# Attention written for both heads of a pair, with fixed PSUM banks and one maximum and exponential over all keys

## The reference

```python
sc = jnp.einsum('bqhd,bkhd->bhqk', qblk, k, preferred_element_type=jnp.float32) * scale
p = jax.nn.softmax(sc, axis=-1).astype(v.dtype)
return jnp.einsum('bhqk,bkhd->bqhd', p, v)
```

## The kernel before, in words

| Stage | Heads, in pairs | Keys | Rows of a score matmul | Units |
|---|---|---|---|---|
| 1, `attn` | 8 as (0,4), (1,5), (2,6), (3,7) | 512 | 64, in the lower or upper half of the partitions | 32 |
| 2, `ca` | 4, alone | 256 | 128 | 16 |
| 3, `mla` | 8 in pairs | 512 + 256 | 96 | 32 |
| 4, `na` | 8 in pairs | 512 + 256 | 64, lower or upper half | 32 |

## Time and profile before

### The profile page before, as it was taken

One profiled execution on the slowest core, in us unless ns is written; L12 is line 12 of the kernel. 1 busy time (PEld: TensorE's weight loads), 2 busy tenths in 40 slices (PEclk: granted clock), 3 DMA queues, 4 the chain that ended last, 5 costly groups with the idle time before them and its releaser, 6 DMA issues.

```text
span 2101.5 us, 21475 instructions
## 1 busy us (share of the span) xinstructions
PE 1892.6 (90%) x8510; PEld 1051.3 (50%) x8510; DVE 676.8 (32%) x1363; ACT 515.6 (25%) x1113; POOL 293.6 (14%) x132
## 2 busy tenths in 40 slices
PE   7999989986989798898979798886999999999988
PEld 5886334464343242434333242423955489546876
DVE  2594765354020100202020110205357500760054
ACT  4242341242010000100010000004346522654231
POOL 2322640300000000000000000002200042004460
PEclk9997799998999999999999999998699999999998
DMA  6230204524999999999999999994210072102131
GB/s 229 65 118 36 80 30 170 167 76 201 424 422 421 421 421 421 421 424 423 424 421 421 421 422 420 424 423 184 81 40 1 5 106 81 41 1 91 41 120 40
DMA packets 97119, 482.15 MB, mean 229 GB/s; under 512 B 21572, under 2 KB 26020, under 8 KB 79648
## 3 DMA queue, kind: packets, MB, share of 16 engines
q1 hardware_dynamic: 96016, 478.84, 57.5%
q0 software_dynamic: 1040, 2.46, 0.6%
HBM read 477.22 MB, written 4.55 MB: 229 GB/s over the span
## 4 chain that ended last, share of the span: by engine, by line
PE 67%; DVE 12%; DMA 11%; SPq 5%; issue 2%; ACT 2%; DVEq 0%; ACTq 0%
PE psum L492 33%; PE psum L1558 14%; DMA ring<-in_expert_w_down 10%; PE psum L1578 7%; SPq L1497 5%; PE psum L1541 3%; PE psum L573 3%; PE psum L1587 3%; PE psum L2123 2%; DVE ring L633 1%; DVE work_area L884 1%; DVE work_area L989 1%; DMA ring<-in_w_mod 1%; DVE work_area L1630 1%; DMA ring<-in_ca_wo 0%
## 5 line engine op out<-in xcount | busy, mean ns | idle before, releaser
L1558 PE MATMUL psum<-ring,work_area 128*64 128x512 f32 x2048 | 448.1, 594 | 35.9 <-DMA ring<-in_expert_w_gu 28.1
L1558 PEld LDWEIGHTS psum<-ring,work_area 128*64 128x64 f32 x2048 | 148.0, 137 | 329.5 <-issue 277.1
L1578 PE MATMUL psum<-ring,work_area 128*64 128x512 f32 x1024 | 233.4, 607 | 26.2 <-DMA ring<-in_expert_w_down 24.2
L1647 DVE TENSOR_TENSOR work_area<-psum,work_area 128x512 f32<-128x512 f32 x32 | 20.6, 686 | 595.0 <-ACT work_area L1610 595.0
L492 PE MATMUL psum<-ring 128*64 128x512 f32 (+3 forms) x384 | 173.3, 597 | 5.3 <-DVE small L1031 2.7
L1578 PEld LDWEIGHTS psum<-ring,work_area 128*64 128x64 f32 x1024 | 74.1, 139 | 175.2 <-issue 147.0
L492 PE MATMUL psum<-ring,hn 128*128 128x512 f32 (+4 forms) x384 | 151.7, 532 | 3.5 <-ACT work_area L604 1.1
L1744 POOL TENSOR_TENSOR hn<-x_res,ring 128x1024 f32<-128x1024 f32 x3 | 7.0, 2362 | 1046.2 <-DVE x_res L1654 1046.2
L1698 POOL TENSOR_TENSOR block_lo<-ring,part_hi 128x1024 fp32r<-128x1024 f32 x36 | 85.9, 2394 | 407.4 <-ACT part_hi L1691 407.4
L1610 ACT ACTIVATE work_area<-psum 128x512 f32<-128x512 f32 x32 | 17.4, 595 | 485.6 <-PE psum L1558 485.6
L492 PEld LDWEIGHTS psum<-ring,hn 128*128 128x128 f32 (+2 forms) x384 | 67.7, 188 | 80.3 <-issue 72.5
(11 more groups left out here) (408 smaller groups left out, 2833.4 us busy)
## 6 DMA issues: line engine op xcount, KB each, us to landing
ring<-in_expert_w_gu SPq DMA_DIRECT2D x128, 2048.0 KB, 26.1
ring<-in_expert_w_down SPq DMA_DIRECT2D x64, 2048.0 KB, 22.7
ring<-in_w_in SPq DMA_DIRECT2D x12, 2048.0 KB, 7.9
ring<-in_w_mod SPq DMA_DIRECT2D x8, 1536.0 KB, 6.5
ring<-in_w_out SPq DMA_DIRECT2D x3, 2048.0 KB, 13.1
ring<-in_ca_wkv SPq DMA_DIRECT2D x1, 4096.0 KB, 16.5
work_area<-na_scratch SPq DMA_DIRECT2D x16, 224.0 KB, 6.7
ring<-in_w_in SPq DMA_DIRECT2D x3, 1024.0 KB, 18.1
```

The lines of the kernel that those rows point to most:

```text
L1558: ins = pe.matmul(psum[h * 64:(h + 1) * 64, c, :], xsT[:, k, e * CAP:(e + 1) * CAP], w[:, (2 * c + h) * BANK:(2 * c + h + 1) * BANK], star ...
L1578: ins = pe.matmul(psum[n * 64:(n + 1) * 64, 6, :], hidT[b][:, j, h, :], w[:, j, n * BANK:(n + 1) * BANK], start=(q == 0 and j == 0), stop= ...
```

## The change

The helper plans by pairs. Units alternate between the two heads of a pair, and a step O covers two blocks of queries of both heads (256 columns each) where it covered four blocks of one. PE writes the scores of both units of a pair segment by segment in turn (`scores_pe`), and the value products of both heads in turn, into the lower and the upper 64 partitions (`out_pe`). PSUM is no longer a circle: banks 0 to 3 hold scores, 4 to 6 turned weights, 7 the outputs. A unit with 768 keys takes two score banks, so two units fit, and two turning banks with three blocks each. The maximum and the exponential run once over the unit's whole width, across banks; in stage 4 the maximum and exponential keep their two parts, because of the bias. Semaphores for scores, exponentials, turns and copies take the place of the bank semaphores, and at its start each stage waits until banks 0 to 6 are drained. Stage 2 has single heads and so the same units as before.

```diff
@@ -49,7 +49,8 @@
 NSLOT = 8
 NEG = -1e30
 SMALL = 672
-O_LATER = 3
+O_LATER, LAG = 3, 3
+SCORE_BANKS, TURN_BANKS, OUT_BANK = 4, (4, 5, 6), 7
...
-        def plan_attention(heads, segs, nkt, lag):
-            units = [(c, j, qt) for c in range(len(heads)) for j in range(len(heads[c])) for qt in range(T)]
-            order, n_out = [], 0
...
+        def plan_attention(heads, width):
+            nj = len(heads[0])
+            quarter = T // nj
+            units = [(c, part * quarter + q, j) for c in range(len(heads)) for part in range(nj)
+                     for q in range(quarter) for j in range(nj)]
+            n, order, turned, n_out = len(units), [], 0, 0
+            for i in range(0, n + nj * LAG, nj):
+                order += [("S", u) for u in range(i, min(i + nj, n))]
+                while turned < min(i + nj - LAG, n) or (i + nj >= n + nj * LAG and turned < n):
+                    order.append(("T", turned))
+                    turned += 1
+                while (n_out + 1) * T + O_LATER <= turned or (turned == n and n_out < n // T):
                     order.append(("O", n_out))
                     n_out += 1
-            size = {"S": len(segs), "T": -(-nkt // 4), "O": 1}
-            return units, order, {(kind, i): list(B.take(size[kind])) for kind, i in order}
...
+            banks_each = -(-width // BANK)
+            n_scores, per_turn = SCORE_BANKS // banks_each, nkt // banks_each
+            starts = [sum(segs[:i]) for i in range(nseg)]
+            def score_at(u):
+                o = (u % n_scores) * banks_each * BANK
+                return flat[:, o:o + width]
+            def turn_at(m):
+                return psum[:, TURN_BANKS[m % len(TURN_BANKS)], 0:per_turn * P]
...
+            entry = [B.last(b) for b in range(OUT_BANK)]
+            g_out = [B.take_at(OUT_BANK) for n in range(len(units) // T)]
...
+            B.next = 0
+            def scores_pe(first):
+                for s in range(nseg):
+                    for u in range(first, first + nj):
+                        c, qt, j = units[u]
+                        if s == 0 and u >= n_scores:
+                            pe.wait_ge(exped, before + u - n_scores + 1)
+                        ins = pe.matmul(score_at(u)[:, starts[s]:starts[s] + segs[s]], q_at(heads[c][j], qt), k_at(heads[c][j], s),
+                                        start=True, stop=True)
+                        if s == nseg - 1:
+                            ins.then_inc(scored, 1)
+            def turn_pe(u):
+                pe.wait_ge(normed, before + u + 1)
+                for m in range(u * banks_each, (u + 1) * banks_each):
+                    if m >= len(TURN_BANKS):
+                        pe.wait_ge(taken, turns_before + m - len(TURN_BANKS) + 1)
+                    for k in range(per_turn):
+                        o = (m % banks_each * per_turn + k) * P
+                        ins = pe.transpose(turn_at(m)[:, k * P:(k + 1) * P], pbuf[u % np_][:, o:o + P], ident)
+                    ins.then_inc(turned, 1)
+            def out_pe(n):
+                g = g_out[n]
+                B.acquire(pe, g)
+                pe.wait_ge(taken, turns_before + (n + 1) * T * banks_each)
+                for k in range(nkt):
+                    for j in range(nj):
+                        c = units[n * T][0]
+                        ins = pe.matmul(B.at(g)[j * dv:(j + 1) * dv, 0:cols], v_at(heads[c][j], k),
+                                        turns_at(n)[:, j, k, :], start=(k == 0), stop=(k == nkt - 1), skip_group_check=True)
+                B.filled(ins, g)
...
+                        act.wait_ge(maxed, before + i + 1)
+                        p = pbuf[i % np_]
+                        if bias is None:
+                            if i >= np_:
+                                act.wait_ge(turned, turns_before + (i - np_ + 1) * banks_each)
+                            act.activation(p, score_at(i), ACT.Exp, bias=neg_max(i),
+                                           accum_out=sums(i)[:, 0:1]).then_inc(exped, 1)
...
+                        n, q, j = i // T, i % T // nj, i % nj
+                        if i % T == 0 and n >= len(ptbuf):
+                            B.full(act, g_out[n - len(ptbuf)])
+                        for m in range(banks_each):
+                            act.wait_ge(turned, turns_before + i * banks_each + m + 1)
+                            act.activation(turns_at(n)[:, j, m * per_turn:(m + 1) * per_turn, q * P:(q + 1) * P],
+                                           turn_at(i * banks_each + m).rearrange("p (k q) -> p k q", k=per_turn),
+                                           ACT.Identity).then_inc(taken, 1)
...
+                        c, qt, j = units[i]
+                        dve.wait_ge(scored, before + i + 1)
+                        if bias is None:
+                            dve.tensor_reduce(neg_max(i), score_at(i), AX, ALU.max, negate=True).then_inc(maxed, 1)
```

More of the change, by code:

```diff
@@ L97, in __init__, with take_at, last @@
         self.free_sem = [ctx.enter_context(nc.semaphore(f"bank_free{b}")) for b in range(NBANK)]
+        self.used = [0] * NBANK
         self.next = 0
     def take(self, n):
-        g = self.next
-        self.next += n
-        return range(g, g + n)
+        return [self.take_at(None) for _ in range(n)]
+    def take_at(self, bank):
+        if bank is None:
+            bank = self.next
+            self.next = (bank + 1) % NBANK
+        g = self.used[bank] * NBANK + bank
+        self.used[bank] += 1
+        return g
+    def last(self, bank):
+        return (self.used[bank] - 1) * NBANK + bank
     def at(self, g):
@@ new lines, in build, with attention @@
+        units_before, turn_count = [0], [0]
+        def attention(heads, segs, q_at, k_at, v_at, dv, pbuf, ptbuf, o_out, bias=None, besides={}):
+            width, nseg = sum(segs), len(segs)
+            nkt, np_ = width // P, len(pbuf)
+            nj, units, order = plan_attention(heads, width)
+            cols = S // nj
+            flat = psum[:].rearrange("p b c -> p (b c)")
+            banks_each = -(-width // BANK)
[6 more added lines that the diff above has]
+                return psum[:, TURN_BANKS[m % len(TURN_BANKS)], 0:per_turn * P]
+            scored, exped, maxed, normed = sem("at_scores"), sem("at_exp"), sem("at_max"), sem("at_weights")
+            turned, taken, exp_biased = sem("at_turned"), sem("at_taken"), sem("at_exp_biased")
+            before = units_before[0]
+            units_before[0] += len(units)
@@ L557, in on_pe @@
             def on_pe():
-                for s, n in ready:
-                    pe.wait_ge(s, n)
+                for g in entry:
+                    B.drained(pe, g)
                 for kind, i in order:
-                    gs = gid[kind, i]
                     if kind == "S":
-                        c, j, qt = units[i]
-                        for si, g in enumerate(gs):
-                            B.acquire(pe, g)
-                            B.filled(product(g, B.at(g)[:, 0:segs[si]], [(q_at(heads[c][j], qt), k_at(heads[c][j], si))]), g)
+                        if i % nj == 0:
+                            scores_pe(i)
@@ L608, in on_act @@
                     elif kind == "T":
[L609 to L619 removed]
+                        n, q, j = i // T, i % T // nj, i % nj
[6 more added lines that the diff above has]
+                                           ACT.Identity).then_inc(taken, 1)
             def on_dve():
                 def divide(i):
+                    dve.wait_ge(exped, before + i + 1)
+                    s = sums(i)[:, 0:1]
                     if bias is not None:
                         dve.wait_ge(exp_biased, i + 1)
[L626 to L629 removed]
                         link(dve.tensor_tensor(recip(i)[:, 0:1], sums(i)[:, 0:1], sums(i)[:, 1:2], ALU.add))
@@ L1526, in piece @@
             return slot(s)
-        before_experts = range(B.next - NBANK, B.next)
+        before_experts = [B.last(b) for b in range(NBANK)]
         def experts_pe():
```

121 lines of the change are left out of this document (34 added, 87 removed).

## The result

| | before | after |
|---|---|---|
| Median of 4 runs each | 2102.14 us (2100.62 to 2106.4) | 2176.23 us (2169.52 to 2182.35) |
| Span of the profiled execution | 2101.5 | 2176.4 |
| PE, DVE, ACT busy | 1892.6, 676.8, 515.6 | 1851.0, 655.0, 511.3 |
| Mean granted clock | 0.955 | 0.928 |

The account below looks back on a forecast made before the run. PE's own work was taken to bound stage 3, DVE's pace between O's stage 4, POOL parts of stage 1. Span 2101.5 + 30 (stages) + 38 (clock) = 2169.5, plus 0.65 to the median: 2170 us, range 2150 to 2195.

Parts of the forecast that it names:

- The closed loop: Stages 3 and 4: a pair's fourth turning group waits for ACT's copy of the first; 6.76 and 7.35 us a pair.
- Stage 3 +22: Stage 3 at unchanged clock: a period of 16.7 us against 13.28, so 22 us more in all.
- stage 4 +23: Stage 4 at unchanged clock: a period of 17.85 us against 14.45, so 23 us more in all.
- Stage 2's +0.5: Stage 2 keeps its units and pace; waiting for drained banks at the stages' starts adds 0.5 us.
- Clock +38: Stages 3 and 4: pauses in every pair lower PE's clock, costing 38 us, with ends 0 and 120.
- a third of the 120: Stages 3 and 4: share taken of the 120 us that running fully at 1.2 GHz would cost.
- The rival that the clock holds (2132): Stages 3 and 4: the pauses don't lower the clock, so only the +30 remains, 2132 us; chance 0.17.
- Stage 1 -15: Stage 1: no such loop, shorter periods in its free part and a shorter end; 15 us less.
- O and the scores: Column halves overlap in O (3.15 us, stages 3 and 4); row halves in scores (1.28 stage 1, 1.71 stage 4).
- The rival without overlap of row halves (2187): Stages 1 and 4: row halves don't run side by side, 2187 us; chance 0.17 together with a lower-clock case.
- The rival "faster" (2068): Stages 3 and 4: the copy isn't in the loop, 5.1 us a pair, period about 12.2; 2068 us, chance 0.05.

Follow-up runs that it names:

- e1: Changed kernel, but in stages 3 and 4 ACT copies the first turned row between the two exponentials, not behind both: 2105.0 us.
- e9: Changed kernel, but turned rows and the values' product share one ring of four PSUM banks: 2131.18 us.
- e5: Changed kernel, but in stage 3 alone the scores of a pair are issued row by row: 2148.57 us.
- e10: Changed kernel, but in stages 3 and 4 DVE takes both maxima of a pair before the two divisions: 2150.31 us.
- e8: Changed kernel with scores row by row, maxima first, copies between the exponentials and one ring of four banks: 2061.34 us.
- e12: Changed kernel with the third group's transposes repeated to fill PE's pause, 6 times in stage 3 and 11 in stage 4: 2143.78 us.
- e3: Changed kernel, but stages 3 and 4 have the order, banks and instructions of the kernel before: 2082.63 us.
- e7: Changed kernel, but in stage 3 maximum and exponential are taken in two parts as before: 2208.43 us.

## Why the prediction was right

Forecast 2170, measured 2176.23: the sum was 68 over the span before, the spans differ by 74.9. By its own terms:

- **The closed loop: right, with its numbers.** Predicted for stage 3 a pair of 6.76 us, a pause of 2.9, an O of 3.15, a period of 16.7; measured at full clock 6.83, 2.63, 2.74 and 16.4 (2 x 6.83 + 2.74). For stage 4: 7.35, 3.8, 17.85; measured 7.35, 4.17, 17.63. The term that was clearly too high is O, by 0.4 us: the 0.38 that I added for tile switches doesn't show in its rows. One reading was wrong and cost little: in stage 4 before, I took DVE's 2.28 us a unit for its own pace, but PE's rows there have no idle time either and start 2.29 apart (1835.18, 1837.47); after the change DVE goes from one unit to the next in 2.20 (1862.05 to 1864.25). That the copy is the link is shown by e1 (moved: 71 us less) and e9 (wait taken away: 45 us less).
- **Stage 3 +22, stage 4 +23: right, low in stage 4.** Measured with the pause filled: +23.2, and at most +29.5 in stage 4, at 0.95 of the clock. Stage 2's +0.5 fits as well: from the end of stage 1 to the start of stage 3 it is 0.6 us longer (1248.9, 1249.5).
- **Clock +38: right in size.** Filling the pause gives back 15.8 us in stage 3 and 19.8 in stage 4, 35.6 together. That a pause lowers the clock was read off a row; that it costs a third of the 120 was a guess between far ends from one row, and that the sum came out so near is in part luck. The third means some 20 us for each stage. Worked out from their means, stage 3, at 0.84, was at half clock for 32% of its time and lost 15.8 us; stage 4, at 0.73, for 54%, and lost at least 19.8. In stage 3 the clocks of e1 (a pause of 1.04: 0.98), e5 (1.77: 0.96), e10 (1.92: 0.87) and after (2.63 and 2.00: 0.84) fall with the pause. But the pause alone doesn't set the clock: stage 4 had 0.80 in e1 with pauses of 2.0 and 1.6 us, and 0.86 in e8 with 1.26 and 0.36. What else sets it stays open. The rival that the clock holds (2132) is what e12 measures with the pause filled, 2144, so it was 12 us low even on its own ground. The Trainium skill's TensorE: Matmul & The Clock Gate, "A second HAM failure mode: psum-queue depth-cycling", says that idle pieces between groups as a kernel goes round its PSUM buffers make the clock go up and down; this case agrees, with 0.84 and 0.73.
- **Stage 1 -15: right** (-17.1). In its free part PE's period fell from 10.14 to 6.93 us (248.65 to 255.58, start of one O to the next), where I had 7.1; e3 shows that the gain reaches the end whole.
- **O and the scores: overlap confirmed.** 24 rows in 2.81 us; 8 rows of scores in 1.57 in stage 4 and 4 in 1.13 in stage 1. To the next start these are 1.50 and 1.06 us, for which I took 1.71 and 1.28, so both were 0.2 too high; the words beside the 1.71 (one row of 256 behind the first half's 1.28) give 1.49. The rival without overlap of row halves (2187) is out.
- **The rival "faster" (2068): its mechanism exists, its number was wrong.** With the copies between the exponentials the pair's loop is 5.36 us, not 5.1, but O does not hide in it: the period is 13.4, not 12.2, because the fourth group still waits for a copy. The step from 5.1 to 12.2 was not worked out, and its gains don't follow from it: 8 periods of 12.2 save 8.6 us in stage 3 and 18 in stage 4, where I wrote 7 and 12. It needed three more changes (e8) to get to 2061.

What the prediction didn't see is how much stands beside the named link. I credited one exponential over all keys with 0.4 us a row "inside the sums"; inside a closed loop that also steers the clock, e7 puts it at 32 us. The order of scores within a pair, which I listed as a given, is worth 28.

```profile
248.65 1.95 PE L628 MATMUL psum<-ring 128*64 128x256 f32 x16
250.53 1.13 PE L603 MATMUL psum<-ring 64*128 64x512 f32 x4
...
255.02 0.63 PE L617 MATMUL psum<-const_sb,ring 128*128 128x128 f32 x4 [0.69 <-ACT ring L672]
255.58 1.95 PE L628 MATMUL psum<-ring 128*64 128x256 f32 x16
```

These rows are PE in stage 1 after the change: the same code, but two groups a pair for three banks, and the wait for a copy is 0.69 us.

## What to carry to other kernels

When buffers of a ring are fixed, count the groups that one step of the order asks of it: if that is more than there are buffers, the step holds a wait on itself, and everything between the first group's arrival and its reader's turn, on every engine, is on the path. Look then at what stands ahead of that reader in its engine's order; moving two copies, 0.86 us together, ahead of one exponential was worth 71 us here. A pause of that kind is paid twice where it lowers TensorE's clock, once as time and once as slower work: here 53 and 36 us in the two long stages.

## What the runs showed of the hardware

- Transposes, put where PE stood still, kept TensorE's clock up: 270 more of them took it from 0.84 to 0.99 in stage 3, and 495 more from 0.73 to 0.95 in stage 4.
- Two halves of the array, by rows or by columns, overlapped for four rows of work (two float32 matmuls) on each side of a change of heads. Row halves: two matmuls of one head and then two of the other took 1.57 us, as when alternated; a single head's two took 1.55 before. Column halves: 12 rows of one and 12 of the other took 4.59 us, alternated 2.81; the second head's first row started beside the ninth of the first head's twelve, and in stage 1 beside the fifth of eight. Longer runs of row halves were not tried.
- The reduction over 768 columns of PSUM across a bank's border takes 0.96 us, the exponential 0.90, against 0.69 + 0.42 and 0.69 + 0.46 in two parts: one instruction across two banks had no extra price here.
